# Long convolutions by FFT: planes forward and back in batches of four, with four forward banks and one merged copy

## What is computed

```python
def bidir_long_conv(u, h_fwd, h_bwd):
    seqlen = u.shape[1]
    k = jnp.concatenate([h_fwd[:1] + h_bwd[:1], h_fwd[1:], jnp.zeros_like(h_fwd[:1]),
                         jnp.flip(h_bwd[1:], axis=0)], axis=0)
    u_f = jnp.fft.rfft(u, n=2 * seqlen, axis=1)
    k_f = jnp.fft.rfft(k, n=2 * seqlen, axis=0)
    return jnp.fft.irfft(u_f * k_f[None], n=2 * seqlen, axis=1)[:, :seqlen]

def hyena_mixer(proj, conv_w, conv_b, ...):
    ...
    z = v
    for o, gate in enumerate((x1, x2)):
        z = gate * (bidir_long_conv(z, filt[:, 0, o], filt[:, 1, o]) + h_bias[o] * z)
    return z
```

## Time and profile before

| what | value |
|---|---|
| median of 3 runs (lowest, highest) | 3526.19 us (3524.51, 3526.88) |
| the profiled execution, its span | 3527.49 us, 3525.4 us |
| PE, PE weight load busy in the span | 3236.5 us (92%), 2608.0 us (74%) |
| DVE, ACT, POOL busy in the span | 2108.2, 1452.4, 1958.0 us |
| ACT copy `conv_v` x128 (L1665) | 126.4 us |
| DVE product x120 (L1696) | 141.7 us, 1220 ns each |
| POOL `conv_both` x256 (L1506, L1507) | 187.0 us, 731 ns each |

### The profile page before, as it was taken

One profiled execution on the slowest core, in us unless ns is written; L12 is line 12 of the kernel. 1 busy time (PEld: TensorE's weight loads), 2 busy tenths in 40 slices (PEclk: granted clock), 3 DMA queues, 4 the chain that ended last, 5 costly groups with the idle time before them and its releaser, 6 DMA issues. The chain is left out here.

```text
span 3525.4 us, 55788 instructions
## 1 busy us (share of the span) xinstructions
PE 3236.5 (92%) x21878; PEld 2608.0 (74%) x21878; DVE 2108.2 (60%) x2493; ACT 1452.4 (41%) x2709; POOL 1958.0 (56%) x1324
## 2 busy tenths in 40 slices
PE   7899999999799999996779989999778997999998
PEld 3677888887588888885569866667566886788886
DVE  6787886223896893222744345555586775667662
ACT  4433223334333223333247745555447763333332
POOL 0486999777787998772100025343467763444542
PEclk9999999999899999998889989999989998999998
DMA  8444333333343333334899864764665665566562
GB/s 297 154 146 154 110 108 120 108 114 108 100 154 113 117 108 119 108 114 157 322 287 298 267 156 130 168 154 120 228 256 174 199 186 192 195 208 195 187 191 99
DMA packets 530472, 592.22 MB, mean 168 GB/s; under 512 B 287403, under 2 KB 408131, under 8 KB 527171
## 3 DMA queue, kind: packets, MB, share of 16 engines
q1 hardware_dynamic: 438957, 430.82, 40.6%
q10 hardware_dynamic: 91256, 157.83, 12.1%
HBM read 383.76 MB, written 204.80 MB: 167 GB/s over the span
## 5 line engine op out<-in xcount | busy, mean ns | idle before, releaser
L759 PE MATMUL pl_bank<-hl_hi,pl_a_hi 128*128 128x512 f32 x2056 | 812.8, 395 | 42.8 <-DVE hl_lo L391 30.2
L761 PE MATMUL pl_bank<-hl_hi,pl_a_lo 128*128 128x512 f32 x2056 | 804.4, 391 | 0.0
L760 PE MATMUL pl_bank<-hl_lo,pl_a_hi 128*128 128x512 f32 x2056 | 803.8, 391 | 0.0
L704 POOL TENSOR_TENSOR pl_a_lo<-hl_early_x,pl_a_hi 128x512 fp32r<-128x512 f32 x288 | 434.2, 1519 | 117.0 <-ACT pl_a_hi L808 116.9
L759 PEld LDWEIGHTS pl_bank<-hl_hi,pl_a_hi 128*128 128x128 f32 x2056 | 388.0, 189 | 129.8 <-DVE hl_lo L391 29.0
L761 PEld LDWEIGHTS pl_bank<-hl_hi,pl_a_lo 128*128 128x128 f32 x2056 | 388.0, 189 | 82.2
L760 PEld LDWEIGHTS pl_bank<-hl_lo,pl_a_hi 128*128 128x128 f32 x2056 | 388.6, 189 | 78.0
L808 ACT ACTIVATE pl_a_hi<-hl_early_x 128x512 fp32r<-128x512 f32 x288 | 182.0, 633 | 541.6 <-PE pl_bank L761 452.7
L2271 POOL TENSOR_TENSOR mo_w_lo<-mo_w,mo_w_hi 128x1024 fp32r<-128x1024 f32 x96 | 238.7, 2488 | 276.1 <-ACT mo_w_hi L2342 276.1
L704 POOL TENSOR_TENSOR pl_a_lo<-hl_w,pl_a_hi 128x512 fp32r<-128x512 f32 x220 | 312.0, 1432 | 114.4 <-ACT pl_a_hi L808 114.3
L2299 PE MATMUL mo_bank<-mo_hi,mo_w_hi 128*128 128x512 f32 x768 | 305.3, 398 | 22.3 <-POOL mo_w_lo L2271 17.6
(11 more groups left out here) (236 smaller groups left out, 6082.1 us busy)
## 6 DMA issues: line engine op xcount, KB each, us to landing
hl_w<-in_w_rec SPq DMA_DIRECT2D x146, 512.0 KB, 3.6
mo_w<-in_w_br SPq DMA_DIRECT2D x96, 512.0 KB, 3.7
kern_s<-taps_res SPq DMA_DIRECT2D x16, 2048.0 KB, 7.0
spec_s<-spec_res ACTq DMA_DIRECT2D x128, 256.0 KB, 3.8
conv_spec<-spec_s SPq DMA_DIRECT2D x240, 128.0 KB, 2.8
g_s<-pl_res ACTq DMA_DIRECT2D x32, 512.0 KB, 2.6
spec_xin<-kern_s SPq DMA_DIRECT2D x32, 512.0 KB, 6.2
spec_xin<-kern_s SPq DMA_DIRECT2D x128, 128.0 KB, 3.8
```

Source lines behind the costliest of these rows:

```text
L704: nc.gpsimd.tensor_tensor(a_lo[:, at % NS, :], src, a_hi[:, at % NS, :].bitcast(F32), ALU.subtract).then_inc(s_lo, 1)
L759: pe.matmul(out, a_hi[:, q, m], op_hi[:, b, k, :], start=begin, stop=False)
L760: pe.matmul(out, a_hi[:, q, m], op_lo[:, b, k, :], start=False, stop=False)
L761: return pe.matmul(out, a_lo[:, q, m], op_hi[:, b, k, :], start=False, stop=end)
```

## The change

All of it is in `phase_long_convs`. `ubank` gets a fourth bank, `forward` and `product` use `h % 4`. PE works off the plane loop in batches of four planes, with `forward` of planes 4 to 7 ahead of the first `inverse`, and both of the next convolution's first `first` ahead of the last batch of four. Two planes of `inverse` (a `pair`) now share a pair of banks, h even in the left 256 columns, h odd in the right 256; ScalarE copies both with one instruction of 1024 elements per partition. `s_vm` counts pairs. The wait for the last `gate` moves from plane 1 to plane 2 of `inverse`. VectorE's, GpSimd's and SP's orders stay.

```diff
-        ubank = (front[1][:, 0], front[1][:, 1], front[0][:, 1])
+        ubank = (front[0][:, 0], front[0][:, 1], front[1][:, 0], front[1][:, 1])
...
                 elif j:
-                    pe.wait_ge(s_p, NH * j - 1 + q)
+                    pe.wait_ge(s_p, NH * j - 2 + 2 * q)
...
                 if q == 0:
-                    pe.wait_ge(s_vm, NH * (j + 1))
+                    pe.wait_ge(s_vm, NH // 2 * (j + 1))
...
-                if h >= 3:
-                    pe.wait_ge(s_p, NH * j + h - 2)
+                if h >= 4:
+                    pe.wait_ge(s_p, NH * j + h - 3)
...
             def inverse(j, h):
                 n = NH * j + h
-                if h >= 2:
-                    pe.wait_ge(s_vm, n - 1)
+                pair = h // 2
+                if pair >= 2:
+                    pe.wait_ge(s_vm, NH // 2 * j + pair - 1)
+                elif j and pair:
+                    pe.wait_ge(s_gate, NR * j)
                 elif j:
                     pe.wait_ge(s_te, NQ * j)
-                    if h == 1:
-                        pe.wait_ge(s_gate, NR * j)
...
-                        mm = pe.matmul(inv[:, 2 * (h % 2) + pl, 0:CB], wv[rows, h, a, :], both[rows, n % PS, a, :], start=(a == 0), stop=(a == 1))
+                        mm = pe.matmul(inv[:, 2 * (pair % 2) + pl, h % 2 * CB:(h % 2 + 1) * CB], wv[rows, h, a, :],
+                                       both[rows, n % PS, a, :], start=(a == 0), stop=(a == 1))
...
-                    for h in range(0, NH, 2):
-                        if h == NH - 2 and j + 1 < NV:
+                    for h in range(4, 8):
+                        forward(j, h)
+                    for b in range(0, NH, 4):
+                        if b == NH - 4 and j + 1 < NV:
                             first(j + 1, 0)
                             first(j + 1, 1)
-                        inverse(j, h)
-                        inverse(j, h + 1)
-                        if h + 4 < NH:
-                            forward(j, h + 4)
-                            forward(j, h + 5)
+                        for h in range(b, b + 4):
+                            inverse(j, h)
+                        for h in range(b + 8, min(b + 12, NH)):
+                            forward(j, h)
...
-                        act.wait_ge(s_v, n + 1)
-                        nc.scalar.copy(v[:, :, 2 * h:2 * h + 2].rearrange("p c k -> p k c"),
-                                       inv[:, 2 * (h % 2):2 * (h % 2) + 2, 0:CB]).then_inc(s_vm, 1)
+                        act.wait_ge(s_v, NH * j + 2 * pair + 2)
+                        nc.scalar.copy(v[:, :, 4 * pair:4 * pair + 4].rearrange("p c (e k) -> p e k c", e=2),
+                                       inv[:, 2 * (pair % 2):2 * (pair % 2) + 2, :].rearrange("p k (e c) -> p e k c", e=2)
+                                       ).then_inc(s_vm, 1)
```

More of the change, by code:

```diff
@@ L1562, in forward @@
                         pe.wait_ge(s_p, NH * j)
-                if h >= 3:
-                    pe.wait_ge(s_p, NH * j + h - 2)
+                if h >= 4:
+                    pe.wait_ge(s_p, NH * j + h - 3)
                 for a in range(2):
                     for pl in range(2):
-                        mm = pe.matmul(ubank[h % 3][pl * NA:(pl + 1) * NA, a * CB:(a + 1) * CB],
+                        mm = pe.matmul(ubank[h % 4][pl * NA:(pl + 1) * NA, a * CB:(a + 1) * CB],
                                        wf[:, 2 * h + pl, a * NA:(a + 1) * NA], y[:, 2 * h + pl, :], start=True, stop=True)
@@ L1656, in _ @@
                 if j < NV:
-                    for h in range(NH):
-                        n = NH * j + h
-                        if h == NH - 2 and j + 1 < NV:
+                    for pair in range(NH // 2):
+                        if pair == NH // 2 - 2 and j + 1 < NV:
                             taken(j + 1, 0)
                             taken(j + 1, 1)
-                        if h == 0 and j:
+                        if pair == 0 and j:
                             act.wait_ge(s_t, NQ * j)
-                        act.wait_ge(s_v, n + 1)
-                        nc.scalar.copy(v[:, :, 2 * h:2 * h + 2].rearrange("p c k -> p k c"),
-                                       inv[:, 2 * (h % 2):2 * (h % 2) + 2, 0:CB]).then_inc(s_vm, 1)
+                        act.wait_ge(s_v, NH * j + 2 * pair + 2)
+                        nc.scalar.copy(v[:, :, 4 * pair:4 * pair + 4].rearrange("p c (e k) -> p e k c", e=2),
+                                       inv[:, 2 * (pair % 2):2 * (pair % 2) + 2, :].rearrange("p k (e c) -> p e k c", e=2)
+                                       ).then_inc(s_vm, 1)
         @block.vector
@@ L1683, in product @@
                 n = NH * j + h
-                u = ubank[h % 3].rearrange("p (a c) -> p a c", a=2)
+                u = ubank[h % 4].rearrange("p (a c) -> p a c", a=2)
                 dve.wait_ge(s_u, n + 1)
```

## The result

| | before | after |
|---|---|---|
| median of 9 runs (lowest, highest) | 3526.19 us (3524.51, 3528.71) | 3536.36 us (3531.28, 3537.38) |
| the profiled execution, its span | 3527.49 us, 3525.4 us | 3536.65 us, 3534.9 us |
| PE busy in the span | 3236.5 us | 3230.2 us |

The change makes the kernel slower: ratio 1.0025, 95% interval 1.0016 to 1.0034. That is +8.8 us by the ratio (5.6 to 12.0), +10.2 by the medians. PE does less (6.3 us less busy time) and the kernel takes longer, so the loss is waiting.

A forecast was written before the change was run, and what follows sets the result against it. PE was taken to bound the plane loops. Undisturbed loops -3.0, three loops waiting for DMA +2.6, +2.2 and +1.8, the clock +1.7: +5.3 us, 3531.5 us in all, +0.15%; range 3518 to 3542.

The forecast's parts named there:

- Switches: PE's plane loop: each change between `forward` and `inverse` costs about 0.16 us; 7 of 12 go, 1.1 us saved.
- Rival D: The 0.16 us belongs to each pair of planes, so batches save nothing: 3540.3 us; chance 0.1.
- Plane 1's wait: Plane 1 of `inverse` no longer waits for the last `gate`: 0.42 us saved in a plane loop.
- The copy: ScalarE's merged copy out of `inv` takes 1.9 us, so PE waits 1.15 us ahead of `turn`, before 0.13.
- Rival B: A cheap merged copy, with the stalls for spectra: 6.4 us less, 3525.1 us; chance 0.1.
- An undisturbed loop: Plane loops that don't wait for DMA, five of eight: about 0.6 us less each, -3.0 us together.
- First loop: First convolution: work behind product 7, partly at half clock, puts `turn` at 2093.7 against 2091.90: +1.8 us.
- Fourth loop: Fourth convolution: the last `inverse` batch stands behind product 15's late spectrum; `turn` at 2265.9 against 2263.30: +2.6 us.
- Fifth loop: Fifth convolution: late spectra hold the last four `inverse` planes; `turn` at 2325.7 against 2323.48: +2.2 us.
- The clock: Half clock after PE's gaps ahead of the last `inverse` batch, fourth and fifth convolution; counted once: +1.7 us.
- A: Rival: the spectra come in time, so all eight plane loops gain 0.6 us: 3521.4 us; chance 0.2.
- C: Rival: ScalarE's last two copies become the bound at the loop's end: 3535.2 us, or near 3549; chance 0.2.

The follow-up runs named there:

- pairs_merged: The changed kernel with merged copy and four forward banks, but PE's old order of two planes of each kind by turns: 3531.33 us, ratio 1.0011.
- sp3_after: The changed kernel with SP's queue reordered so late loads of `x`, gates and edges stand behind nearly all spectra: 3508.54 us, ratio 0.995.
- sp3_before: The kernel before the change with SP's queue reordered, late loads of `x`, gates and edges behind nearly all spectra: 3517.35 us, ratio 0.9976.

## Why the prediction was right

The sign of the sum was right, and 3536.36 lies in the range of 3518 to 3542. The size was short: +5.3 us or +0.15% was forecast, within the 0.2% of no change, and +0.25% was measured, beyond it. So the outcome is the "slower" that had the chance 0.39, and not the "same" that had 0.49. Step by step:

- **Switches.** Right. 3.60 and 3.66 us for four planes, against 3.62 and 3.67. Rival D falls.
- **Plane 1's wait.** Right: in pairs_merged planes 0 and 1 of `inverse` take 2177.88 to 2179.81 = 1.93 us, not 2.35, and its sum above closes with the 0.42.
- **GpSimd and VectorE.** Right. In the third loop PE shows no idle time until `turn`, in spite of the 0.2 us of slack.
- **The copy.** Taken as 1.9, measured 1.97 on average and 3.68 for two back to back. That decided between the rows: the 1066 ns of the old copy scaled, the 588 ns form did not. By the Trainium skill (ScalarE: Activation LUTs, What ACT_TABLE_LOAD costs) it would be an estimated 1.04 us; the trace disagrees by 0.93. The Trainium skill's rule in SBUF — State Buffer (Door 1: The DMA port swizzle), a penalty for each access that crosses into another 16-byte line, agrees in direction; the page gives no size for it. Rival B falls.
- **An undisturbed loop.** Forecast -0.6, measured -0.78: `turn` waited 0.97 where 1.15 was laid out, mainly because the last two copies took 3.68 us together and not 3.80. Five loops gave -3.9 instead of -3.0.
- **First loop.** Its `turn` was put at 2093.7 and came at 2093.34. (The loop reads 2.86 longer because it also began 1.42 us earlier, while the spectrum landed when it did before.)
- **Fourth loop.** `turn` was put at 2265.9 and came at 2268.67. Of the 2.8 us, 1.1 are the landing: product 15 was done at 2259.37 + 1.22 = 2260.59, not 2259.45, as planes 14 and 15 landed apart. That the landing times stay where they are held within 0.2 us for product 12 (2253.69 against 2253.88) and failed by 1.1 for the last. The other 1.6 are the clock: 0.4 on the `first`, 1.2 on `inverse` and what follows.
- **Fifth loop.** It began 5.38 us later than before; product 15 was done 0.3 us sooner after that than forecast, `turn` came 1.9 later. That is the clock's share, below.
- **The clock, the step that failed.** "I count one: +1.7". Both loops had it: 1.6 us in the fourth, and in the fifth 0.5 on the `first` (2324.36 to 2325.43 = 1.07, where 0.55 was laid out) and 7.55 - 5.91 = 1.6 from there to `turn`. So this term is 3.7 us and not 1.7. (Against the 5.78 us that the undisturbed loop takes there, and not the 5.91 laid out, it is 4.0.) The rows at hand, and the earlier trace rows, had shown half clock behind 2.06 us without work; both waits were forecast at over 2 us, and there was no reason to count one alone.

The sum of the plane phase: against the forecast, -0.9 (undisturbed), -0.4 (first), +2.9 (fourth), +1.9 (fifth), -1.7 (the forecast's term for the clock, whose measured cost is in the two before) and -0.8 us (transforms between the loops, 145.85 to 145.02, not forecast) make +1.0. That errors of up to 2.9 us leave so little is luck. Indeed the last of the eight `turn` marks moved from 2492.8 to 2499.1, +6.3 against +5.3. The rest of the difference lies behind it, in code that the change doesn't touch: 1032.6 us before, 1035.8 after. That stretch was between 1031.2 and 1037.0 in the profiled executions of all thirteen kernels, and neither a row nor a run says why. So some 3 us of the 8.8 to 10.2 stay open.

**The rivals.** A (the spectra come in time) is not what happened, yet sp3_after shows that it was the right condition: given that, the change gains 8.8 us over sp3_before. C (ScalarE as the bound at the loop's end) is true in part: it holds `turn` for 0.97 us in each loop, but at 1.97 us a copy the loop still gains. That C's 3535.2 us lies nearer to the measured time than the forecast does is chance. The stalls decided the sign.

## What to carry over

A tighter order on the bounding engine also moves up when it asks for data. Before counting its gain, look in the loader's queue for what stands ahead of each load, in the loops where slack hides it today; reordering that queue was worth more here (11.7 us in the medians by itself, 13.1 in the plane loops) than the change (8.8 us once the queue was right, 6.4 in the loops), and fixing only as much as the old order needs leaves the new one waiting. A load that is moved back can itself come late: look at who needs it next. Count a wait of some us on TensorE at its length and again at what half clock takes from the work behind it, for every place where it occurs. When two small copies are merged, take the price from copies of the same access pattern: the merged one took 1.97 us against 2 x 1.07 and made `turn` wait; what it bought was room for four planes in the same banks.

## What the runs showed of the hardware

- **Copies with a step.** The copy of 512 fp32 elements per partition to places 32 elements apart took 1066 ns on ScalarE, one of 1024 took 1970 ns: 1.77 ns for each further element, and a copy of 512 contiguous ones takes 588 in all. Beside each other on the two halves, VectorE (1.14 to 1.18 us for 512) was no quicker than ScalarE.
- **The clock around a wait.** In three places PE stood still and the granted clock then was 0.50 (1.2 GHz) for a stretch. Fourth loop: a wait of 3.62 us up to 2260.65, half clock 2260.90 to 2264.30, all of it on work. Fifth loop: a wait of 4.38 us up to 2324.36, half clock 2322.30 to 2329.10, so 2.06 us of it in the wait and 4.7 on work. First loop: a wait of 9.80 us up to 2072.75, half clock 2066.30 to 2076.50, 3.75 us of it on work. Four planes of `inverse` took 4.97, 5.46 and 4.57 us in those places, 3.66 otherwise. Why the clock fell ahead of the work in one place and behind it in another isn't shown.
- **Transfers in one queue.** With no byte more or less (592.22 MB in both), moving the seven loads of gates and `x` that stood ahead of plane 7's spectrum to later places took the first loop from 41.05 to 33.03 us. With `next_x` moved too, VectorE's waits for spectra fell from 17.9 to 0.4 us over the eight loops.
